# The decay products of an SSD stage, made in one fp32 pass or in two fp32r passes over split step sizes

## The reference, cut to what matters

```
A = jnp.transpose(a_dt.reshape(b, nc, SSD_CHUNK, g, r), (0, 3, 4, 1, 2))
A_cs = jnp.cumsum(A, axis=-1)
Lm = segsum_exp(A)                                   # exp of sums of A between two tokens
cb = jnp.einsum('bclgn,bcsgn->bgcls', Cc, Bc)
y_diag = jnp.einsum('bgrcls,bcsgrp->bclgrp', cb[:, :, None] * Lm, X)
...
y_off = jnp.einsum('bclgn,bcgrpn,bgrcl->bclgrp', Cc, prev_states, jnp.exp(A_cs))
```

## Time and profile before

| | us |
|---|---|
| median of 3 runs (2672.66 to 2673.99) | 2673.97 |
| the profiled execution | 2673.27 |
| its span in the profile | 2671.0 |
| TensorE busy in the span | 2443.0 (91%) |
| VectorE busy | 1499.8 (56%) |
| GpSimd busy | 269.9 (10%) |

### The profile page before, as it was taken

The page is one execution under the profiler, slowest core; times in us unless marked ns, Lnnn a source line. Parts: engine busy times, 40 slices in busy tenths (PEclk is TensorE's granted clock), DMA queues, the critical chain, the costliest instruction groups (busy, mean ns, idle before and its releaser), DMA issues.

```text
span 2671.0 us, 37241 instructions
## 1 busy us (share of the span) xinstructions
PE 2443.0 (91%) x15721; PEld 2175.4 (81%) x15721; DVE 1499.8 (56%) x2267; ACT 785.1 (29%) x1319; POOL 269.9 (10%) x269
## 2 busy tenths in 40 slices
PE   6899889989998898869999998799999879999995
PEld 3768658878887888849999998686666869999995
DVE  3375562287228764576634652796666476615644
ACT  3433332200220053232322222333444242222321
POOL 0021130033004301110000001100000210000002
PEclk9999999999999999979999999898999989999997
DMA  7402115400530022202222222111000212222221
GB/s 288 142 24 68 55 52 205 174 9 9 205 142 9 5 91 64 100 19 72 79 79 72 72 80 64 38 57 35 1 1 1 64 32 72 72 81 70 79 79 40
DMA packets 44293, 193.71 MB, mean 73 GB/s; under 512 B 5057, under 2 KB 5057, under 8 KB 37345
## 3 DMA queue, kind: packets, MB, share of 16 engines
q1 hardware_dynamic: 40752, 175.48, 19.3%
q0 software_dynamic: 2224, 13.24, 1.4%
q10 hardware_dynamic: 1152, 2.62, 0.2%
HBM read 183.72 MB, written 7.60 MB: 72 GB/s over the span
## 4 chain that ended last, share of the span: by engine, by line
PE 81%; DVE 14%; ACT 2%; issue 1%; DMA 0%; POOL 0%; SPq 0%; DVEq 0%; ACTq 0%
PE pg L479 59%; PE ps L632 3%; PE pg L768 3%; PE ps L793 3%; DVE rb L1196 2%; PE ps L781 2%; PE ps L506 2%; DVE xT L1239 2%; PE ps L448 1%; DVE hl L1202 1%; DVE att L1368 1%; DVE wk L1374 1%; PE ps L575 1%; PE ps L579 1%; PE ps L596 1%
## 5 line engine op out<-in xcount | busy, mean ns | idle before, releaser
L479 PE MATMUL pg<-hh,whi 128*128 128x320 f32 x2992 | 713.6, 320 | 78.1 <-DVE hl L1202 65.0
L479 PE MATMUL pg<-hl,whi 128*128 128x320 f32 x2992 | 690.4, 312 | 0.0
L479 PE MATMUL pg<-hh,wlo 128*128 128x320 f32 x2992 | 689.0, 312 | 0.0
L479 PEld LDWEIGHTS pg<-hh,whi 128*128 128x128 f32 x2992 | 503.8, 191 | 144.0 <-issue 114.9
L1176 DVE TENSOR_TENSOR wlo<-ring,whi 128x1024 fp32r<-128x1024 f32 x231 | 282.9, 1225 | 451.2 <-ACT whi L836 451.0
L479 PEld LDWEIGHTS pg<-hl,whi 128*128 128x128 f32 x2992 | 508.8, 191 | 0.0
L479 PEld LDWEIGHTS pg<-hh,wlo 128*128 128x128 f32 x2992 | 508.2, 191 | 0.0
L836 ACT CAST whi<-ring 128x1024 fp32r<-128x1024 f32 x231 | 241.8, 1047 | 312.7 <-PE pg L479 273.9
L632 PE MATMUL ps<-wk,kg 128*128 128x128 f32 x1120 | 160.5, 294 | 26.0 <-DVE wk L1374 18.2
L632 PEld LDWEIGHTS ps<-wk,kg 128*128 128x128 f32 x1120 | 140.6, 199 | 45.6 <-DVE wk L1374 37.6
L1196 DVE RECIPROCAL rb<-rt 128x640 f32<-128x640 f32 x29 | 120.4, 4152 | 76.8 <-ACT rt L857 76.8
(11 more groups left out here) (243 smaller groups left out, 2929.0 us busy)
## 6 DMA issues: line engine op xcount, KB each, us to landing
ring<-in_wstream SPq DMA_DIRECT2D x231, 512.0 KB, 3.6
adaring<-in_wada SPq DMA_DIRECT2D x21, 1024.0 KB, 5.1
ybuf<-in_wada SPq DMA_DIRECT2D x21, 1024.0 KB, 4.9
adabig<-in_wada SPq DMA_DIRECT2D x6, 1024.0 KB, 18.7
xT<-in_x SPq DMA_DIRECT2D x1, 2560.0 KB, 11.0
yssd_scratch<-ybuf POOLq DMA_DIRECT2D x2, 1280.0 KB, 6.2
xT<-yssd_scratch POOLq DMA_DIRECT2D x1, 2560.0 KB, 10.8
xT<-in_x POOLq DMA_DIRECT2D x1, 2560.0 KB, 10.8
```

What stands on the lines that cost most here:

```text
L479: last = nc.tensor.matmul(out[:, half], w[:, s % 2, pos, :], a[:, k, half * HALF:(half + 1) * HALF], start=n == 0 and m == 0, stop=n == le ...
```

## The change

`ra` becomes two arrays. `rah` holds the step sizes rounded to fp32r, times the triangle (VectorE, as before). `ral` holds what the rounding left, times the triangle, and is made on GpSimd by a new function `rest_sizes`. TensorE multiplies both by the triangle in fp32r and adds the two products in PSUM. The 0 and 1 matrices (`cmr`) and the split of `adt` (`adth`, `adtl`) are made once, behind `adt`.

```diff
@@ TensorE, decays
-                        pe.wait_ge(ra_ready, v + 1)
-                        if v:
-                            pe.wait_ge(ex_ready, v)
-                        nc.tensor.matmul(ps[:, 0, :], cm[:, (GT, LT)[d], :], ra[:, d].rearrange("p h t -> p (h t)"),
-                                         start=True, stop=True).then_inc(dd_ready, 1)
-                        if v:
-                            pe.wait_ge(exc_ready, v)
-                        nc.tensor.matmul(ps[:, 1, :], cm[:, ONES, :], ra[:, d].rearrange("p h t -> p (h t)"),
-                                         start=True, stop=True).then_inc(dd_ready, 1)
+                        for bank, m, freed_by in ((0, 1 + d, ex_ready), (1, 0, exc_ready)):
+                            if v:
+                                pe.wait_ge(freed_by, v)
+                            for part, made, r in ((0, rah_ready, rah), (1, ral_ready, ral)):
+                                pe.wait_ge(made, v + 1)
+                                last = nc.tensor.matmul(ps[:, bank, :], cmr[:, m, :],
+                                                        r[:, d].rearrange("p h t -> p (h t)"),
+                                                        start=part == 0, stop=part == 1)
+                            last.then_inc(dd_ready, 1)
@@ VectorE, step_sizes
+                    if u == 0 and d == 0:
+                        dve.wait_ge(cmr_ready, 1)
+                    a = adth[:, t, d * 16 + HPG * g + 4 * q:d * 16 + HPG * g + 4 * q + 4].bitcast(F32)
+                    V.tensor_tensor(rah[:, d], per_head(a, P),
                                     cm[:, (LE, GE)[d], :].unsqueeze(1).broadcast_to([P, 4, P]),
+                                    ALU.mult).then_inc(rah_ready, 1)
@@ VectorE, behind adt
                     dve.wait_ge(dt_ready, 1)
+                    link(V.tensor_copy(adth[:], adt[:]))
+                    V.tensor_copy(cmr[:, 0], cm[:, ONES, :])
+                    V.tensor_copy(cmr[:, 1:3], cm[:, GT:LT + 1, :])
+                    V.tensor_tensor(adtl[:], adt[:], adth[:].bitcast(F32), ALU.subtract).then_inc(cmr_ready, 1)
@@ GpSimd, behind the stores of the prompt's states
+                def rest_sizes(n):
+                    (t, q), u = SSD_UNITS[n], g * len(SSD_UNITS) + n
+                    for d in range(2):
+                        if u:
+                            pool.wait_ge(dd_ready, 4 * (u - 1) + 2 * d + 2)
+                        h0 = d * 16 + HPG * g + 4 * q
+                        G.tensor_tensor(ral[:, d], adtl[:, t, h0:h0 + 4].unsqueeze(2).broadcast_to([P, 4, P]),
+                                        cm[:, (LE, GE)[d], :].unsqueeze(1).broadcast_to([P, 4, P]),
+                                        ALU.mult).then_inc(ral_ready, 1)
+
+                pool.wait_ge(cmr_ready, 1)
+                pool.wait_ge(yd_ready, g + 1)
+                pool.wait_ge(tr_done, 7 * (g + 1))
+                rest_sizes(0)
                 for i, (t, q) in enumerate(SSD_UNITS):
                     u = g * len(SSD_UNITS) + i
+                    if i + 1 < len(SSD_UNITS):
+                        rest_sizes(i + 1)
                     for d in range(2):
                         pool.wait_ge(exc_ready, 2 * u + d + 1)
```

More of the change, by code:

```diff
@@ L192, in hybrid_step @@
         with ExitStack() as ph:
+            with ExitStack() as over:
+                rah = sb("rah", [P, 2, 4, P], F32R, over)
+                ral = sb("ral", [P, 2, 4, P], F32R, over)
             xsT = sb("xsT", [P, 4, NT], F32, ph)
@@ L198, in hybrid_step @@
             st = sb("st", [P, 2, 4, 512], F32, ph)
-            ra = sb("ra", [P, 2, 4, P], F32, ph)
+            adth = sb("adth", [P, TT, 32], F32R, ph)
+            adtl = sb("adtl", [P, TT, 32], F32, ph)
+            cmr = sb("cmr", [P, 3, P], F32R, ph)
             eg = sb("eg", [P, 2, 4, P], F32, ph)
@@ L323, in hybrid_step @@
         cb_ready = sem("cb_ready")
-        ra_ready = sem("ra_ready")
+        rah_ready = sem("rah_ready")
+        ral_ready = sem("ral_ready")
+        cmr_ready = sem("cmr_ready")
         dd_ready = sem("dd_ready")
@@ L1298, in step_sizes @@
                         dve.wait_ge(dd_ready, 4 * (u - 1) + 2 * d + 2)
-                    a = adt[:, t, d * 16 + HPG * g + 4 * q:d * 16 + HPG * g + 4 * q + 4]
-                    V.tensor_tensor(ra[:, d], per_head(a, P),
+                    if u == 0 and d == 0:
+                        dve.wait_ge(cmr_ready, 1)
+                    a = adth[:, t, d * 16 + HPG * g + 4 * q:d * 16 + HPG * g + 4 * q + 4].bitcast(F32)
+                    V.tensor_tensor(rah[:, d], per_head(a, P),
                                     cm[:, (LE, GE)[d], :].unsqueeze(1).broadcast_to([P, 4, P]),
-                                    ALU.mult).then_inc(ra_ready, 1)
+                                    ALU.mult).then_inc(rah_ready, 1)
                 def add_output(n):
```

## The result

| | before | after |
|---|---|---|
| median, us | 2673.98 (4 runs) | 2691.69 (3 runs, 2690.14 to 2691.83) |
| ratio, with its 95% interval | | 1.0065 (1.0045 to 1.0085) |
| the same kernel, timed again | 2673.8 (18 runs) | 2692.91 (2691.47 to 2694.02, 5 runs) |
| ratio | | 1.0072 (1.0060 to 1.0085) |
| span of the profiled execution | 2671.0 | 2692.2 |

The kernel is slower, by 17.7 us in the first measurement and 19.1 in the second. The forecast was slower by 32.5, with a range from 2694; the sign was right, the size was not.

What follows compares the result with a forecast made beforehand. The prediction took TensorE to bound the units before the change and VectorE's and GpSimd's turns at their shared port after it. Holds +24.6, small operations +1.2 and clock +7 on 2673.27 us gave 2706.5 us, range 2694 to 2722.

Steps and rivals of the forecast that it cites:

- holds of the port: SSD units: VectorE and GpSimd operations with SBUF inputs take turns; the added turns cost +12.3 us per group, +24.6 in all.
- clock: SSD units: TensorE idles, its granted clock falls and VectorE waits for outputs; 3.5 us per group, +7 in all.
- small operations: VectorE behind `adt`: four added operations (split of `adt`, matrix copies) delay the chain once, +1.2 us, between 0.8 and 1.5.
- The chain of this stretch is TensorE from end to end: SSD units before the change, 166 to 226 us: TensorE alone sets the pace, 12.80 us per pair of units.
- The holds, summed: SSD units: 15.0 us of holds per pair against 9.3 of TensorE work; a group takes 79.2 us for 66.9.
- I take 1.12 as a hold: GpSimd's new `ral` operation, 128x512, occupies the shared port for 1.12 us, between 1.09 and 1.49.
- 0.8 us of gaps per group: SSD units: gaps between holds add 0.8 us, taking a group's sum from 78.4 to 79.2 us.
- Faster: Rival, chance 0.05: in the units `ral` takes no turns with VectorE, TensorE bounds again; about 2654 us.
- Clock down through the units: Rival: TensorE stays at 1.2 GHz, +13 us per group, about 2726; chance 0.17 together with the slow `ral`.
- A slow `ral` of 1.49: Rival: GpSimd's `ral` takes 1.49 us in the units, 6.7 more per group, 2719; shares the 0.17 chance.
- L1308 and L1321: VectorE operations in the units, taken to stay out of the turns; otherwise about 1.3 us more per pair, some 11 in all.

Runs made afterwards that it cites:

- fp32-product kernel: Changed kernel with `ral` made but not read and TensorE multiplying `rah` alone, in plain fp32 with the original matrices: 2683.8 us.
- filler: Changed kernel with each `rah` product made three times over the same bank, same result: 2685.58 us.
- e10: Changed kernel with `ral` made on ScalarE, unit 0's ahead of the first exponentials, and the small operations one weight tile later: 2662.5 us.

## Why the prediction was wrong, point by point

| term, both groups | forecast | measured | from |
|---|---|---|---|
| holds of the port | +24.6 | +11.8 | units of the fp32-product kernel (145.6) against those before (133.8) |
| clock | +7 | +6.9 | units: filler (147.5) against changed (154.5) |
| reading `ral` | 0 | +2.0 | units: filler against fp32 product; the filler kernel's clock is 0.97, so part of it is still clock |
| small operations | +1.2 | about +0.8 | L1260 later by 1.22 - 0.42 |
| sum | +32.8 | +21.5 | profiled spans: 2692.2 - 2671.0 = 21.2; medians: 17.7 and 19.1 |

The profiled execution of the changed kernel was the slowest of its five, 1.1 us above their median, so the last row's two measures agree to about 1 us.

- **What bounds.** The step that VectorE and GpSimd take turns, and that this and not TensorE would bound the units, was right. The doubling, the removal and the move of `ral` to VectorE and to ScalarE all follow it. That GpSimd would be nearly full was too strong: it waits 2.82 us for TensorE once in each of the later pairs. And "The chain of this stretch is TensorE from end to end" was misread. Before the change the first pair was already bound by the turns, and TensorE's chain begins behind it:

```profile
165.10 1.67 DVE ra L1300
...
178.91 1.13 PE ps L575 x2
```

The sum for a group doesn't rest on this sentence, since it compares all holds with the measured 66.9 us.
- **The step that failed: "The holds, summed".** Its mechanism was right and its size was not: it gave +24.6, and the turns cost +11.8. The largest part is "I take 1.12 as a hold". A `ral` holds for 0.84 us (0.865 by GpSimd's row), 0.28 less, for 18 in each of two groups: 10.1 us. The argument was that L1694's 0.634 form "is not slow", from which I concluded that a repeated input doesn't matter; that it could be faster was not asked, so the bounds 1.09 to 1.49 reached only upwards. The old products hold for 1.08 and not 1.12 (40 of them, 1.6 us): the prediction's own row had it, 1.76 us for 0.68. And the 0.8 us of gaps per group was not there (1.6 in all). With the three mended the group comes to 79.2 - 5.0 - 0.8 - 0.8 = 72.6 us, against 71.9 in the first group of the kernel with fp32 products, at full clock, and 73.7 in the second. That a pair of the changed kernel takes 15.1 us, close to the 15.3 forecast, is luck: 13.7 are holds, and the rest is the clock and the reading of `ral`, which the 15.3 didn't contain. The whole kernel with fp32 products is only 9.8 us above the kernel before, less than its units and the small operations give (12.6). The rest of the difference lies outside the units, and no run explains it. Last, the sum's end is off by a little: 2706.1 and 0.7 give 2706.8 and not 2706.5.
- **The clock.** +7 forecast, 6.9 measured in the units by the filler (7.3 by the medians). Removing the lower clock in another way, fp32 for fp32r products, gives back 3.9 in the units and 7.6 by the medians. The reason given was right in part: VectorE waits for an output at a lower clock, but the four products ahead of it are slower too (2.04 for 1.17 us). That 3.5 per group fits is partly luck, since it was picked between nothing and 12.5.
- **The rivals.** "Faster" was wrong about its mechanism, `ral` does take turns, but right that a repeated operand needs the port less: 0.84 for 1.08, where 0.4 would have been break-even. "Clock down through the units" came halfway: 0.83, not 0.50. A slow `ral` of 1.49 falls: 1.04 us alone, and 1.10 as a hold even with a full operand.
- **The range.** It began at 2694, from holds of 1.0 us for `ral` without loss of clock. The true hold lay under that end, because the price of an operation that no row showed was bounded from one side only.
- **L1308 and L1321**, which read PSUM, don't take turns: 0.29 us for L1330 inside a GpSimd product. Right.

Still open is why the first and the second group differ by 2 us in the changed kernel (76.2 and 78.3) and in the one with fp32 products (71.9 and 73.7), when before the change both took 66.9. In both kernels the second group also has the lower granted clock (0.80 for 0.83 in the changed one), which goes the same way; why the clock is lower there isn't known.

## What to carry to other kernels

Count the holds of the port that VectorE and GpSimd share before moving work to an idle GpSimd: 0.60 us for VectorE and 0.84 to 1.10 for GpSimd per 128x512 here, so the idle engine was the dearer of the two, and ScalarE, off that port, was the right place. Making TensorE shorter in a stage that another engine bounds gained nothing here and lost clock: compare the granted clock of the stage before and after. Bound the price of an operation that no row shows from below as well as from above.

## What was not expected of the hardware

- A slower product made the kernel faster: 2683.8 us with fp32 against 2691.37 with fp32r (3.9 us of it in the units), at a granted clock of 1.00 against 0.77 in the units.
- Useless matmuls gain 7.3 us where TensorE idles (clock 0.83 to 0.97) and lose 8.4 where it has little room.
- A GpSimd product 128x512 whose one operand is four numbers, each repeated 128 times, takes 1.04 us when it has not to wait and holds the port for 0.84 to 0.865; with a full operand in its place it holds it for 1.10.
- ScalarE writes a 128x128 product with a scale per partition every 0.30 us (8 in 2.44 us), and takes no turns with VectorE: in e10 such eight, from 193.82 us, take 2.44 us, and a VectorE operation inside them (195.85) takes 0.68.
